# State-space stage of a hybrid layer: GpSimd takes the skip term D times x, VectorE's two sums change places, chunks are turned back two later, and SyncE loads the exponent rows

## The reference

```python
def ssd_chunked(x, dt, a, bm, cm, init_state):
    ...
    seg = a_cs[..., :, None] - a_cs[..., None, :]
    lmat = jnp.exp(jnp.where(causal, seg, -jnp.inf))
    cb = jnp.einsum("bclgn,bcsgn->bgcls", cc, bc)
    y_diag = jnp.einsum("bgcls,bgrcls,bcsgrp->bclgrp", cb, lmat, xr)
    ...
    y_off = jnp.einsum("bclgn,cbgrpn,bgrcl->bclgrp", cc, entering, jnp.exp(a_cs))
    y = (y_diag + y_off).reshape(b, l, h, p)

# in ssm_mixer
y = y_f + flip(y_b) + d_skip.astype(f32)[:, None] * xs.astype(f32)
y = y.reshape(b, l, SSM_WIDTH) * jax.nn.silu(z.astype(f32))
return rms_norm(y, g_out).astype(z.dtype), fin_f, fin_b
```

## Time and profile before

| | |
|---|---|
| median of 3 runs | 1667.59 us (1666.72 to 1667.93) |
| the profiled execution, its time | 1670.06 us |
| its span in the profile | 1668.2 us |
| granted TensorE clock over the span | 0.994 |
| PE busy | 1621.0 us (97%) |
| DVE busy | 1017.8 us (61%) |
| ACT busy | 705.7 us (42%) |
| POOL busy | 100.4 us (6%) |
| the loop over chunks | from about 350 to 428 us of the span |

### The profile page before, as it was taken

The page is one execution under the profiler, slowest core; times in us unless marked ns, Lnnn a source line. Parts: engine busy times, 40 slices in busy tenths (PEclk is TensorE's granted clock), DMA queues, the critical chain, the costliest instruction groups (busy, mean ns, idle before and its releaser), DMA issues. The chain is left out here.

```text
span 1668.2 us, 25023 instructions
## 1 busy us (share of the span) xinstructions
PE 1621.0 (97%) x9735; PEld 1414.1 (85%) x9735; DVE 1017.8 (61%) x1689; ACT 705.7 (42%) x1288; POOL 100.4 (6%) x123
## 2 busy tenths in 40 slices
PE   6999999999899999999999999999999999999997
PEld 4787878877688988878889999999999998888886
DVE  4653645268655555554587656666665665477788
ACT  4632112357554444545664333333333334434453
POOL 1101000013000000320000000000000000000011
PEclk9999999999999999999999999999999999999999
DMA  9324441013200000323312222212222226663445
GB/s 372 149 98 145 158 155 52 1 56 105 74 20 1 14 1 1 108 89 133 127 51 87 97 80 93 106 73 98 91 97 81 92 81 219 232 217 97 126 162 191
DMA packets 76294, 176.36 MB, mean 106 GB/s; under 512 B 10353, under 2 KB 26945, under 8 KB 74129
## 3 DMA queue, kind: packets, MB, share of 16 engines
q1 hardware_dynamic: 72080, 169.75, 29.3%
q0 software_dynamic: 4096, 5.01, 0.9%
HBM read 131.02 MB, written 43.70 MB: 105 GB/s over the span
## 5 line engine op out<-in xcount | busy, mean ns | idle before, releaser
L374 PE MATMUL psF<-gv,gu_ring 128*128 128x384 f32 (+1 forms) x664 | 220.6, 332 | 3.9 <-DVE gv L2748 3.2
L375 PE MATMUL psF<-gv,gu_ring 128*128 128x384 f32 (+1 forms) x664 | 220.1, 332 | 0.0
L376 PE MATMUL psF<-gv,gu_ring 128*128 128x384 f32 (+1 forms) x664 | 220.1, 331 | 0.0
L381 PE MATMUL psF<-gv,gu_ring 128*128 128x512 f32 x540 | 193.6, 392 | 0.0
L382 PE MATMUL psF<-gv,gu_ring 128*128 128x256 f32 x540 | 151.3, 280 | 0.0
L374 PE MATMUL psF<-d_w_ring,d_hid_ring 128*128 128x512 f32 x360 | 140.2, 389 | 0.0
L375 PE MATMUL psF<-d_w_ring,d_hid_ring 128*128 128x512 f32 x360 | 140.1, 389 | 0.0
L376 PE MATMUL psF<-d_w_ring,d_hid_ring 128*128 128x512 f32 x360 | 140.1, 389 | 0.0
L374 PEld LDWEIGHTS psF<-gv,gu_ring 128*128 128x128 f32 x664 | 125.3, 189 | 10.4 <-issue 3.6
L375 PEld LDWEIGHTS psF<-gv,gu_ring 128*128 128x128 f32 x664 | 125.5, 189 | 0.0
L374 PE MATMUL psP<-hT_hi,win_hi 128*128 128x512 f32 (+1 forms) x336 | 123.7, 368 | 1.8 <-DVEq L1085 1.5
(11 more groups left out here) (457 smaller groups left out, 3704.3 us busy)
## 6 DMA issues: line engine op xcount, KB each, us to landing
hid_variants<-hraw SPq DMA_DIRECT2D x77, 320.0 KB, 2.2
d_hid<-hid_variants SPq DMA_DIRECT2D x58, 320.0 KB, 3.0
m_wring<-in_w_mod SPq DMA_DIRECT2D x16, 1024.0 KB, 4.9
d_b<-in_w_down SPq DMA_DIRECT2D x44, 256.0 KB, 4.5
win_raw<-in_w_in SPq DMA_DIRECT2D x18, 512.0 KB, 5.7
w_mod_staged<-in_w_mod SPq DMA_DIRECT2D x16, 512.0 KB, 15.3
d_hid_more<-hid_variants SPq DMA_DIRECT2D x19, 320.0 KB, 3.2
raw_gu<-in_w_gate SPq DMA_DIRECT2D x11, 512.0 KB, 3.8
```

What stands on the lines that cost most here:

```text
L374: pe.matmul(out, w_hi, x_hi, start=first, stop=False, skip_group_check=onto)
L375: pe.matmul(out, w_hi, x_lo, start=False, stop=False, skip_group_check=onto)
L376: return pe.matmul(out, w_lo, x_hi, start=False, stop=last, skip_group_check=onto)
L381: pe.matmul(both, w_hi, x_both, start=first, stop=False, skip_group_check=onto)
```

## The change

- **The skip term leaves TensorE.** The 4 products with `ddiag` go, and so do the 4 ScalarE operations that made `ddiag`. During the gate tiles GpSimd multiplies x of every chunk by D (10 operations `xd`, 128x512, into the room of the transposed input). In the loop it adds `xd` to the backward part alone (`carried`, after `off_b_read`, signals `y_summed`).
- **VectorE's sums change places.** The addition of the backward part stands behind `next_state` and the two `wt` operations, and waits for `y_summed`.
- **Turned two later.** TensorE turns chunk c - 2 in iteration c where it turned c - 1. ScalarE goes square(c - 1), exponents(c + 1), weigh(c + 1), mix(c - 2), scale(c - 1). The square gets a junk tile of its own.
- **SyncE loads u.** Chunks 0 and 1 are still loaded by GpSimd ahead of the loop, chunks 2 and 3 by SyncE ahead of it; the load for chunk c + 4 stands in SyncE's loop behind the wait for `mix_ready` of chunk c and the store of that chunk. The copy that makes u rounds it first, since SyncE's transfer cannot convert.

```diff
@@ -540,7 +541,7 @@
         sb_in = lambda c: in_lo[:, 0:4, chunk(c)]
         bt = lambda c: in_lo[:, 4:6, chunk(c)]
         per_head = lambda ap: ap.rearrange("p (a r) -> p a r", r=2).unsqueeze(3).to_broadcast([P, 4, 2, SP_])
-        dskip = L.cols[:, C_DS:C_DS + 4]
+        xd = lambda c: L.xbcT[:, 0:4, chunk(c)]
         up2 = L.up2
         psF = psP[:].rearrange("p a b n -> p (a b) n")
         Q = psF[:, 0:4, :]
@@ -614,6 +615,13 @@
             sp.wait_ge(kv_stored, 16)
             sp.wait_ge(kr_stored, 16)
             sp.wait_ge(q_stored, 16)
+
+            def load_u(c):
+                sp.wait_ge(seg_done, c - 1)
+                sp.dma_start(pick[64:66, c % 2, :, :].bitcast(F32), L.u_s[:, :, chunk(c)]).then_inc(u_later[c % 2], 16)
+
+            load_u(2)
+            load_u(3)
             for c in range(NT):
                 if c >= 1:
                     sp.wait_ge(mix_stored, 16 * c)
@@ -625,6 +633,8 @@
                 if c < NT - 1:
                     sp.wait_ge(mix_ready, c + 1)
                     sp.dma_start(quads(L.mixS[c]), zt(c)).then_inc(mix_stored, 16)
+                if c + 4 < NT:
+                    load_u(c + 4)
 
         @block.gpsimd
         def _(pool):
@@ -690,23 +701,27 @@
                 p.link(pool.tensor_scalar(ms[:, c:c + 1], ss[:, c:c + 1], 1.0 / SW, EPS, ALU.mult, ALU.add))
                 pool.tensor_tensor(rs[:, c:c + 1], ms[:, c:c + 1], nh[:], ALU.pow).then_inc(rstd_ready, 1)
 
-            def load_u(c):
-
-                if c >= 2:
-                    pool.wait_ge(seg_done, c - 1)
-                pool.dma_start(pick[64:66, c % 2, :, :], L.u_s[:, :, chunk(c)]).then_inc(u_loaded[c % 2], 16)
-
             until(pool, tiles[-1])
-            load_u(0)
-            load_u(1)
+            for c in range(2):
+                pool.dma_start(pick[64:66, c, :, :], L.u_s[:, :, chunk(c)]).then_inc(u_loaded[c], 16)
+
+            pool.wait_ge(kr_stored, 32)
+            for i, c in enumerate(down):
+                pool.wait_ge(x_copied, 2 * i + 1)
+                p.mark(pool.tensor_tensor(heads4(xd(c)), heads4(xs(c)), per_head(dskip), ALU.mult))
+            p.wait()
+
+            def carried(c):
+
+                pool.wait_ge(off_b_read, c + 1)
+                pool.tensor_tensor(quads(off_b[:]), quads(off_b[:]), xd(c), ALU.add).then_inc(y_summed, 1)
 
             pool.wait_ge(s_ready, NS)
             for c in range(NT):
                 decay(c)
+                carried(c)
                 if c >= 1:
                     rstd(c - 1)
-                if c + 2 < NT:
-                    load_u(c + 2)
             rstd(NT - 1)
 
         @block.scalar
@@ -844,9 +859,6 @@
                 elif i == 5:
                     act.activation(up2[64:66, :], L.ones[64:66, 0:1].to_broadcast([2, T]), ACT.Copy
                                    ).then_inc(ones_set, 1)
-                elif i == 6:
-                    for a in range(4):
-                        act.activation(ddiag[:, a, :], L.ident, ACT.Copy, scale=dskip[:, a:a + 1]).then_inc(consts, 1)
 
             act.wait_ge(conv_read, N_XBC)
             for i in range(NT):
@@ -860,12 +872,14 @@
             def square(c):
                 act.wait_ge(y_ready, c + 1)
                 if c >= 1:
-                    act.wait_ge(y_turned, c)
-                act.activation(yn[:], yv[:, c % 2, :], ACT.Square, accum_out=ss[:, c:c + 1]).then_inc(squared, 1)
+                    act.wait_ge(squared, c)
+                act.activation(sq_junk[:], yv[:, c % 2, :], ACT.Square, accum_out=ss[:, c:c + 1]).then_inc(squared, 1)
 
             def scale(c):
                 act.wait_ge(rstd_ready, c + 1)
                 act.wait_ge(squared, c + 1)
+                if c >= 1:
+                    act.wait_ge(y_turned, c)
                 act.activation(yn[:], yv[:, c % 2, :], ACT.Copy, scale=rs[:, c:c + 1]).then_inc(yn_ready, 1)
 
             def exponents(c):
@@ -896,11 +910,12 @@
                     square(c - 1)
                 if c + 1 < NT:
                     exponents(c + 1)
+                    weigh(c + 1)
+                if c >= 2:
+                    mix(c - 2)
                 if c >= 1:
                     scale(c - 1)
-                    mix(c - 1)
-                if c + 1 < NT:
-                    weigh(c + 1)
+            mix(NT - 2)
             square(NT - 1)
             scale(NT - 1)
             mix(NT - 1)
@@ -984,7 +999,7 @@
             def take_u(n):
                 which, c = U_PIECES[n]
                 dve.wait_ge(u_turned, n + 1)
-                dst = (u2, L.up2)[which]
+                dst = (u2.bitcast(F32R), L.up2)[which]
                 dve.tensor_copy(dst[0:64, c * P:(c + 2) * P], (psD, psE)[n % 2][0:64, :]).then_inc(u_read, 1)
 
             dve.wait_ge(cond_ready, 1)
@@ -1159,14 +1174,13 @@
                                   ).then_inc(off_f_read, 1)
                 dve.tensor_tensor(heads(off_b[:]), heads(A[2]), across(eoff[:, c, 8:16], SP_), ALU.mult
                                   ).then_inc(off_b_read, 1)
-                dve.wait_ge(off_f_read, c + 1)
-                dve.wait_ge(off_b_read, c + 1)
-                f.link(dve.tensor_tensor(yv[:, c % 2, :], yv[:, c % 2, :], off_b[:], ALU.add))
-
                 if c + 1 < NT:
                     next_state(c)
                     weights_in_chunk(c + 1)
 
+                dve.wait_ge(y_summed, c + 1)
+                dve.wait_ge(off_f_read, c + 1)
+                f.link(dve.tensor_tensor(yv[:, c % 2, :], yv[:, c % 2, :], off_b[:], ALU.add))
                 dve.wait_ge(diag_done, c + 1)
                 f.link(dve.tensor_tensor(yv[:, c % 2, :], yv[:, c % 2, :], A[3], ALU.add))
                 dve.tensor_tensor(quads(yv[:, c % 2, :]), quads(yv[:, c % 2, :]), zt(c), ALU.mult).then_inc(y_ready, 1)
@@ -1384,7 +1398,10 @@
 
                 if c >= 1:
                     pe.wait_ge(exp_done, c)
-                pe.wait_ge(u_loaded[c % 2], 16 * (c // 2 + 1))
+                if c < 2:
+                    pe.wait_ge(u_loaded[c], 16)
+                else:
+                    pe.wait_ge(u_later[c % 2], 16 * (c // 2))
                 for q in range(4) if c else (2, 3, 0, 1):
                     if c == 0 and q < 2:
                         pe.wait_ge(s_ready, NS - 2 + q)
@@ -1399,7 +1416,7 @@
                     mm = pe.transpose(A[0][:, chunk(a)], yn[:, chunk(a)], L.ident)
                 mm.then_inc(y_turned, 1)
 
-            pe.wait_ge(consts, 9)
+            pe.wait_ge(consts, 5)
             pe.wait_ge(ones_set, 1)
             pe.wait_ge(x_copied, 2 * NT - 2)
             pe.wait_ge(z_copied, NT)
@@ -1408,8 +1425,8 @@
 
                 if c >= 1:
                     pe.wait_ge(cb_read, c)
-                if c >= 3:
-                    pe.wait_ge(mix_ready, c - 2)
+                if c >= 4:
+                    pe.wait_ge(mix_ready, c - 3)
                 for g in range(2):
                     mm = pe.matmul(A[0][:, chunk(g)], L.xbcT[:, 4 + g, chunk(c)], L.xbcT[:, 6 + g, chunk(c)],
                                    start=True, stop=True)
@@ -1431,6 +1448,10 @@
                         mm = pe.matmul(A[1 + d][:, g * 256:(g + 1) * 256], L.xbcT[:, 6 + g, chunk(c)],
                                        state[:, 2 * g:2 * g + 2, :], start=True, stop=True)
                 mm.then_inc(off_done, 1)
+                if c == NT - 1:
+                    pe.wait_ge(cb_read, NT)
+                    pe.wait_ge(mix_ready, NT - 3)
+                    y_turn(NT - 3)
                 if c + 1 < NT:
                     segments(c + 1)
                     pe.wait_ge(off_f_read, c + 1)
@@ -1439,21 +1460,20 @@
 
                 if c >= 1:
                     pe.wait_ge(y_ready, c)
-                for a in range(4):
-                    pe.matmul(A[3][:, chunk(a)], L.xbcT[:, a, chunk(c)], ddiag[:, a, :], start=(a == 0), stop=False)
                 pe.wait_ge(w_ready, c + 1)
                 for h in range(SH):
                     for q in range(4):
                         rows = slice(q * P // 4, (q + 1) * P // 4)
                         mm = pe.matmul(A[3][rows, h * SP_:(h + 1) * SP_], wt[:, c % 2, h, rows],
-                                       xs(c)[:, h // 2, (h % 2) * SP_:(h % 2 + 1) * SP_], start=False, stop=(h == SH - 1))
+                                       xs(c)[:, h // 2, (h % 2) * SP_:(h % 2 + 1) * SP_], start=(h == 0), stop=(h == SH - 1))
                 mm.then_inc(diag_done, 1)
-                if c >= 1:
-                    if c + 1 < NT:
-                        pe.wait_ge(cb_read, c + 2)
-                    if c >= 2:
-                        pe.wait_ge(mix_ready, c - 1)
-                    y_turn(c - 1)
+                if 2 <= c < NT - 1:
+                    pe.wait_ge(cb_read, c + 2)
+                    if c >= 3:
+                        pe.wait_ge(mix_ready, c - 2)
+                    y_turn(c - 2)
+            pe.wait_ge(mix_ready, NT - 2)
+            y_turn(NT - 2)
```

19 lines of the change are left out of this document (10 added, 9 removed).

## The result

The kernel after the change takes 1700.40 us in the median of 4 executions (1699.33 to 1701.04), against 1667.68 before (the three runs above and a fourth). The ratio on record is 1.0188, with a 95% interval of 1.0175 to 1.0201: slower by 1.9%. Forecast were 1686, 1679 to 1693. The profiled execution took 1699.78 us, its span is 1698.0 us and its mean granted clock 0.983 (before: 1670.06, 1668.2 and 0.994).

The account below looks back on a forecast made before the run. TensorE was taken to set the pace at 7.38 us a chunk. The circle through the moved load, with loop start and end, added 14.1 us and the falling clock 4.2, so 18.3: 1686 us, range 1679 to 1693.

Parts of the forecast that it names:

- The circle: Loop from chunk 4 on: segments, exponential, scalings, mix, store and load of u in series, 9.58 us a turn against 7.38.
- TensorE's saving: Skip products leaving TensorE in the loop: 0.99 us a chunk, a chunk of TensorE alone falling to 6.39 us.
- The chain that the prediction added up: VectorE and ScalarE in the loop, with gate, square, exponential, weights and two sums in series: 7.2 us a chunk.
- The side: Direction of the whole change: slower at chance 0.91, same 0.05, faster 0.04.
- half clock: TensorE's clock falling to 1.2 GHz around gated segments: 0 to 1.8 us a fall, taken as 0.7, six times, 4.2 us.
- its load's flight: Load of u from SyncE's issue to TensorE: 2.1 plus 0.1, so 2.2 us a turn; ends 1.8 and 2.9.
- start: mix(0): Loop start: iteration 2 put 0.4 us later than 367.53, so mix(0) at 372.7.
- segments(9) to the last mix: End of the loop: 15.56 us before, plus 0.71 for the sum and 1.04 for GpSimd's addition, 17.3.
- a bound of +0.7, once: Gate tiles: the last of GpSimd's ten multiplications can slow a VectorE operation, at most 0.7 us; counted as nothing.
- GpSimd's addition: End of the loop, ahead of the root for chunk 8 that ScalarE waits for: 1.04 us; free within the loop.
- the second (the clock falls ahead of every segments at full price): Gated segments in the loop: 14.1 + 6 x 1.8 = 24.9 us more, so 1692.5; chance 0.12.
- The rival in which the load is no wait and the sum binds: Loop: load of u costs no wait, the moved sum binds at 7.2 us a chunk; 1668.5, no change; chance 0.05.

Follow-up runs that it names:

- Kernels 2: Kernel before with only the load moved: SyncE loads u for chunk c + 4 behind the store of chunk c; 1668.21 us, ratio 0.9993.
- kernel 5: Kernel after, but SyncE loads u for chunk c + 5 behind the store of chunk c, and chunks 2 to 4 ahead of the loop; 1671.94 us, ratio 1.0016.
- kernel 8: kernel 5 with ScalarE's square(c - 1) moved behind exponents(c + 1); 1671.94 us, ratio 1.0017.
- Kernel 3: Kernel after with 14 idle TensorE products ahead of each wait for u from chunk 4 on, results overwritten; 1688.52 us, ratio 1.012.
- Kernel 4: Kernel after with SyncE's load of u issued ahead of the store, still behind the same mix; 1692.23 us, ratio 1.0139.
- kernels 11: kernel 8 with VectorE's gate one iteration later and TensorE's end reordered: last contribution, both turns of y, then final-state transposes; 1668.71 us, ratio 1.0003.
- Kernel 12: The kernel of kernels 11 with SyncE's stores of chunks 7 and 8 issued once mixed, ahead of the previous chunk's landing wait and loads; 1667.08 us, ratio 0.9989.
- kernel 1: Kernel after with only the load's place undone: GpSimd loads u for chunk c + 2 again; 1678.12 us, ratio 1.0055.
- Kernel 10: kernel 8 with VectorE's gate one iteration later and GpSimd's last multiplication by D moved from the gate tiles into the loop; 1671.82 us, ratio 1.0022.

## Why the prediction was right and wrong

**Right: the mechanism.** The circle over segments, exponential, scalings, mix, store and load is there, six times, from chunk 4 on, and chunks 2 and 3 are free of it (7.2 and 7.26 us). Kernels 2 and 5 show it from both sides: the load alone costs nothing, and one chunk more of distance takes nearly all back. Right too that TensorE's saving is worth nothing while the sum is behind the weights: forecast 7.2 us a chunk, measured 7.26 (kernel 5). That the number fits is in part luck. The chain that the prediction added up runs over the square and the exponential, and kernel 8 takes the square out of it and leaves 7.26 as it is; what binds is VectorE's row with its wait for the contribution. The side was right as well.

**Wrong: four terms of the sum, all too small.** The step that failed is the price of the circle: its half clock was put at 4.2 us and measured 10.4, and its load's flight at 2.2 a turn and measured 2.83. The last mix came 31.45 us later, not 18.3. The missing 13.2 us are, from the after trace:

| term | forecast | measured | adds |
|---|---|---|---|
| start: mix(0) | 372.7 | 373.60 | 0.9 |
| mix to load, and flight, six times | 1.15 + 2.2 | 1.22 + 2.83 | 4.2 |
| half clock in the circle and in segments(9) | 6 x 0.7 = 4.2 | 3 x 1.06 + 3 x 2.41 = 10.4 | 6.2 |
| segments(9) to the last mix, without the half clock of the segments | 17.3 | 21.66 - 2.41 = 19.25 | 1.95 |

- **The clock** is the step that failed most. From segments to mix it takes 7.28 and 8.64 us in turn (mean of three each), against 6.23 at full clock. The prediction bounded a fall by the segments alone, 1.8 us, and took 0.7 because the clock would come back while they ran. It never did: in the turns of 7.28 it falls within the segments (products of 0.58, then 0.99) and stays down into the contribution; in those of 8.64 it falls by their first product (0.77, not 0.47) and stays down through the contribution and the scores, so that ScalarE waits another 0.62 us for the scores. So 2.41 lies above the upper bound. Kernel 3 takes the term away: 0.7% of the time, some 11 us. Its trace has 11.6 us less from mix(0) to the mix behind segments(9): the 10.4 of the table, 0.8 of shorter flights (2.69 in the mean) and 0.4 in small differences. At the end of its loop the half clock is still there (0.61 to 0.70 from 440 to 455 us).
- **The flight** was taken at 2.1 us, from a store's landing, where the earlier trace rows had 2.8 for the same transfer on the other queue. That row was the nearest. Kernel 4 shows that the store ahead is not the reason. The estimate of the Trainium skill, DMA: Bandwidth & Descriptors, on the anatomy of one DMA, 2.04 us for 16 KB, is made for GpSimd's path and would be low on SyncE's queue as well: the least seen from issue to the first product is 2.52 (kernel 4).
- **The start**: iteration 2 was taken as 0.4 later than 367.53. It begins at 368.93, which is 1.4 later. Of this, 0.48 is no effect of the change, since the whole execution is that much later ahead of the loop. The moved sum costs 0.70 in the first two iterations (7.19 and 7.26 us, before 6.67 and 7.08), where the prediction had 0.4. The last 0.22 is ahead of the first scaling (9.09 us behind the ScalarE copy, 8.87 before), and it is 9.08 or 9.09 in every kernel with GpSimd's ten multiplications in the gate tiles. From the timeline of POOL and DVE in the kernel after:

```profile
347.59 1.04 POOL L711 TENSOR_TENSOR xbcT<-chunks_hi,d_skip 128x512 f32<-128x512 f32 x1 [3.29 <-ACT chunks_hi L845]
347.82 1.36 DVE L1127 TENSOR_TENSOR xw<-chunks_hi,dt_feats 128x512 f32<-128x512 f32 x1 [0.80 <-ACT chunks_lo L846]
```

  GpSimd's last multiplication comes just ahead of a VectorE operation of the backward sweep, which takes 1.36 us in place of 0.69. The prediction named exactly this as a bound of +0.7, once, and then put it at nothing. The collision is there, but it moves the first scaling by no more than the 0.22.
- **The end.** GpSimd's addition was priced at 1.04 us and takes 1.26. TensorE waits 3.69 us for the scaled chunk 8, which waits for GpSimd's root behind its addition, and after that rest the transposes of the final states and of y run at half clock (1.06 us a group of four, not 0.60 to 0.66), the last of them just ahead of the last mix. The prediction took the last mix for the end of the loop; kernels 11 and 12 show that SyncE's last load can be, and in the kernel after it comes 0.7 later than the last mix.

Of the rivals, the second (the clock falls ahead of every segments at full price) came nearest, with 1692.5; with the flight of 2.83 on top, 6 x 0.63 more, it would have been 1696.3. The range took in each of the two bounds, but not both at once. The rival in which the load is no wait and the sum binds is kernel 5: 0.16% slower where the prediction had 0.05% (1668.5), and its trace says where that lies. Counted from the ScalarE copy, attention starts 3.16 us later than before: 0.22 ahead of the first scaling, 0.70 in the first two iterations, 0.80 gained in the seven others (the rival had 1.26), and 3.04 more from the first scaling of chunk 9 to attention (12.12 us, before 9.08). The rival gave the start 0.4 and the end 1.75.

**What stays open:** why the turns alternate, since the rests ahead of them overlap (2.72, 2.86 and 3.10 us before the short, 2.90, 2.97 and 2.98 before the long), and why in kernel 1 rests of 1.32 and 1.73 us were followed by half clock and rests of 1.42 and 1.56 were not. The length of the rest alone does not order them. Kernel 12 leaves the start as it is.

## What to carry to other kernels

A load in an in-order queue is not only as early as its buffer allows, but as late as everything ahead of it in that queue. When the work that it stands behind is moved an iteration later, its distance must grow by one too: follow the circle from the consumer back to the load, add its rows, and compare the sum with the pace. If the circle is longer, price the rest that it makes by rows at half clock, for all that TensorE does after it until the circle closes. And what is won in a loop is only won if the queue that ends it (here SyncE, with a store, a landing and three loads a chunk) can end earlier too: look for the row that the next phase follows at a fixed distance in several kernels.

## What the runs showed of the hardware

- A rest of 2.7 to 3.1 us, with dense work on both sides, is followed by the clock of 1.2 GHz each of the six times; it cost 1.06 or 2.41 us here. After rests of 1.95 to 2.47 (kernel 4) it was so six times out of six too, in or behind segments, and cost 0.8 to 1.2 us, once 2.3. After rests of 1.3 to 1.7 (kernel 1) it was so two times out of four. With the rest filled by products (kernel 3) the clock is 1.00 in each 5 us of the loop up to 440.
- A load of 16 KB into two partitions lets its consumer go 2.52 to 2.85 us after its issue on SyncE's queue with the store behind it (kernel 4), 2.62 to 2.89 behind a store of 256 KB (kernels 3 and after), and 2.57 to 2.67 four times out of five on GpSimd's queue (kernel 1), where the fifth was 3.67.
- The barrier of all engines ahead of attention ends 0.87 to 0.89 us behind the start of what comes last, in fourteen traces.
- Where GpSimd and VectorE collide with 512 or more columns and two inputs in SBUF each, the one that starts later pays, in each case looked at. In the kernel before, GpSimd's decay came first and kept its 1.04 us, and VectorE's weight operation took 1.96. In the kernel after it is the reverse (timeline of DVE and POOL):

```profile
351.35 1.23 DVE L1152 TENSOR_TENSOR wt<-seg 128x1024 f32<-128x1024 f32 x1
351.39 2.08 POOL L696 TENSOR_TENSOR decayed<-sf,dt_feats 128x512 f32<-128x512 f32 x1 [2.77 <-issue]
352.61 1.95 DVE L1155 TENSOR_TENSOR wt<-wt,cb 128x1024 f32<-128x1024 f32 x1
```

  VectorE started 0.04 us earlier and kept its 1.23; the decay took 2.08, and the next weight operation, which started while the decay ran, 1.95. Kernel 10 has the chain of three: its first weight operation starts behind the decay and takes 2.01, GpSimd's multiplication starts within that and takes 1.89 in place of 1.04, and the second weight operation starts within the multiplication and takes 1.95.
